# Eight expert jobs as one pipeline over the job borders, with the outputs kept in DRAM by slot

## What is computed

```python
logits = (ht @ w_router).astype(jnp.float32)
top_logits, top_idx = lax.top_k(logits, TOP_K)          # TOP_K = 2 of N_EXPERTS = 8
top_w = jax.nn.softmax(top_logits, axis=-1)
combine = jnp.sum(jax.nn.one_hot(top_idx, N_EXPERTS) * top_w[..., None], axis=1)
for e in range(N_EXPERTS):
    y = swiglu(ht, w_gate[e], w_up[e], w_down[e])       # (silu(h @ w_gate) * (h @ w_up)) @ w_down
    out = out + combine[:, e:e + 1] * y
```

## Time and profile before

| | |
|---|---|
| device time, median of 3 (lowest to highest) | 1696.33 us (1695.38 to 1701.48) |
| the profiled execution, from its first to its last instruction | 1695.6 us |
| what lies around that span in the median | 0.7 us |
| TensorE busy | 1564.9 us (92%) |
| VectorE busy | 1245.4 us (73%) |
| ScalarE busy | 1017.5 us (60%) |
| GpSimd busy | 79.7 us (5%) |
| bytes moved | 446.03 MB, 263 GB/s over the span |
| mean granted TensorE clock | 0.962 of full speed |

### The profile page before, as it was taken

One profiled execution on the slowest core, in us unless ns is written; L12 is line 12 of the kernel. 1 busy time (PEld: TensorE's weight loads), 2 busy tenths in 40 slices (PEclk: granted clock), 3 DMA queues, 4 the chain that ended last, 5 costly groups with the idle time before them and its releaser, 6 DMA issues.

```text
span 1695.6 us, 22769 instructions
## 1 busy us (share of the span) xinstructions
PE 1564.9 (92%) x8311; PEld 1308.0 (77%) x8311; DVE 1245.4 (73%) x1044; ACT 1017.5 (60%) x949; POOL 79.7 (5%) x89
## 2 busy tenths in 40 slices
PE   5888999998987877999999999999999999999996
PEld 4777888878986866887887887887887887887885
DVE  4745555545674446888888888888888888888886
ACT  4444434334853334677677677677777777777774
POOL 0002000000223112000000000000000000000000
PEclk9789999999999796999999999999999999999999
DMA  9317655552430212999999999999999999999992
GB/s 329 98 39 275 220 174 194 176 174 100 133 117 28 75 62 97 347 361 351 344 368 349 336 387 337 345 372 344 341 369 351 336 374 349 341 372 339 361 368 88
DMA packets 190790, 446.03 MB, mean 263 GB/s; under 512 B 9632, under 2 KB 10016, under 8 KB 190752
## 3 DMA queue, kind: packets, MB, share of 16 engines
q1 hardware_dynamic: 184032, 430.83, 71.1%
q0 software_dynamic: 3456, 12.58, 1.9%
q10 hardware_dynamic: 3264, 2.08, 0.4%
HBM read 436.03 MB, written 9.44 MB: 263 GB/s over the span
## 4 chain that ended last, share of the span: by engine, by line
PE 84%; DVE 6%; ACT 5%; issue 3%; ACTq 1%; DVEq 1%; POOL 0%; POOLq 0%
PE PS L283 25%; PE PS L285 25%; PE PS L284 25%; DVE w_low L275 2%; ACT w_high L271 2%; PE PS L1277 1%; PE PS L846 1%; PE PS L920 1%; PE PS L1162 1%; ACT xs L520 1%; ACT L271 1%; PE PS L896 0%; PE PS L1153 0%; PE PS L1209 0%; PE PS L909 0%
## 5 line engine op out<-in xcount | busy, mean ns | idle before, releaser
L275 DVE TENSOR_TENSOR w_low<-w_raw,w_high 128x2048 fp32r<-128x2048 f32 x408 | 934.0, 2296 | 247.6 <-ACT w_high L271 247.4
L271 ACT ACTIVATE w_high<-w_raw 128x2048 fp32r<-128x2048 f32 x408 | 781.2, 1917 | 393.9 <-PE PS L285 393.0
L283 PE MATMUL PS<-w_high,x_high 128*128 128x512 f32 x1264 | 503.5, 398 | 23.7 <-DVE pickT L1838 15.1
L285 PE MATMUL PS<-w_high,x_low 128*128 128x512 f32 x1264 | 495.6, 392 | 0.0
L284 PE MATMUL PS<-w_low,x_high 128*128 128x512 f32 x1264 | 494.9, 392 | 0.0
L283 PEld LDWEIGHTS PS<-w_high,x_high 128*128 128x128 f32 x1264 | 239.5, 189 | 76.8 <-DVE w_low L275 22.4
L285 PEld LDWEIGHTS PS<-w_high,x_low 128*128 128x128 f32 x1264 | 238.8, 189 | 51.5
L284 PEld LDWEIGHTS PS<-w_low,x_high 128*128 128x128 f32 x1264 | 239.4, 189 | 48.4
L283 PE MATMUL PS<-w_high,m_act_high 128*128 128x512 f32 x448 | 177.9, 397 | 11.9 <-DVE m_act_low L1831 11.9
L285 PE MATMUL PS<-w_high,m_act_low 128*128 128x512 f32 x448 | 177.2, 395 | 0.0
L284 PE MATMUL PS<-w_low,m_act_high 128*128 128x512 f32 x448 | 177.1, 395 | 0.0
(11 more groups left out here) (271 smaller groups left out, 1364.9 us busy)
## 6 DMA issues: line engine op xcount, KB each, us to landing
w_raw<-in_m_w_gate SPq DMA_DIRECT2D x112, 1024.0 KB, 7.2
w_raw<-in_m_w_up SPq DMA_DIRECT2D x112, 1024.0 KB, 7.1
w_raw<-in_m_w_down SPq DMA_DIRECT2D x112, 1024.0 KB, 6.7
w_raw<-in_b_w_in SPq DMA_DIRECT2D x16, 1024.0 KB, 5.5
w_raw<-in_f_w_gate SPq DMA_DIRECT2D x14, 1024.0 KB, 5.1
w_raw<-in_f_w_up SPq DMA_DIRECT2D x14, 1024.0 KB, 5.1
w_raw<-in_f_w_down SPq DMA_DIRECT2D x14, 1024.0 KB, 4.9
w_raw<-in_a_w_qkv SPq DMA_DIRECT2D x6, 1024.0 KB, 13.9
```

What stands on the lines that cost most here:

```text
L271: nc.scalar.activation(WH[:, n % SPLIT, :], W[:, n % RAW, :], ACT.Copy).then_inc(hi_done, 1)
L275: nc.vector.tensor_tensor(WL[:, n % SPLIT, :], W[:, n % RAW, :], WH[:, n % SPLIT, :].bitcast(f32), ALU.subtract).then_inc(lo_done, 1)
L283: nc.tensor.matmul(o, sH, mH, start=first, stop=False)
L285: return nc.tensor.matmul(o, sL, mH, start=False, stop=last)
```

## The change

The eight jobs become one sequence of 56 chunks, numbered q over all jobs. TensorE does the gate and up of chunk q+1 between the turning and the down of chunk q everywhere but at the end, so over the job borders too. For this the rows of the next job are turned in chunk 5 of a job, after the last up that needs the old ones.

A job's output is no longer carried back by matmuls. ScalarE copies the PSUM banks 2 and 3 to a tile (`y_slots`, `y_out`) in the first chunk of the next job, and GpSimd stores the 512 KB to a DRAM scratch by slot (`y_slots_dram`). In the last job GpSimd gathers each token's two rows with four indirect DMAs (`y_tokens`), and VectorE adds them to `h` with four instructions of 128 x 1024. The last job, whose output isn't stored, and jobs beyond the eighth, if there are any, still go through `back` and `add`. Scratch rows that no stored job writes are cleared with five more stores of zeros, beside the twelve that clear the x scratch. The first up no longer waits for `pickT`, and the reading of `njobs` and its tests come after the eighth job.

```diff
@@ -193,12 +193,17 @@
             w_fin = sb("w_fin", [128, D], c=c)
             m_gain = sb("m_gain", [128, D], c=c)
             xg = sb("x_slots", [128, D], c=c)
+            ys = sb("y_slots", [128, D], c=c)
+            yg = sb("y_tokens", [128, 2, TT, D], c=c)
             late, row_e, row_s = (sb(n, R8, c=c) for n in ("late", "row_e", "row_s"))
             offs = sb("offs", [128, E], c=c)
             rowf = sb("rowf", [128, 2, TT], c=c)
             slot = sb("slot", [128, 2, TT], u32, c=c)
         xw = fin
         x_dram = nc.dram_tensor("x_slots_dram", ((JOBS + 1) * 128, D), f32, kind="Internal").ap()
+        y_dram = nc.dram_tensor("y_slots_dram", ((JOBS + 1) * 128, D), f32, kind="Internal").ap()
+        LAST = E - 1
+        Y_CLEAR = JOBS + 1 - LAST
...
+                def inner(j):
+                    with sp.Fori(0, NC - 1) as i:
+                        gate_up(n0 + 4, j * NC + i, j, ds((i + 1) * CH, CH))
+                        down(n0 + 8, j * NC + i, j, i)
+
+                gate_up(n0, 0, 0, slice(0, CH))
+                with sp.Fori(0, LAST) as j:
+                    inner(j)
+                    gate_up(n0 + 4, j * NC + NC - 1, j + 1, slice(0, CH))
+                    down(n0 + 8, j * NC + NC - 1, j, NC - 1)
+                inner(LAST)
+                down(n0 + 4, E * NC - 1, LAST, NC - 1)
...
+                for j in range(LAST, JOBS + 1):
+                    pool.dma_start(y_dram[128 * j:128 * j + 128, :], zeros[:]).then_inc(sem("y_stored"), 16)
...
+                def store(j):
+                    pool.wait_ge(sem("ys_out"), j + 1)
+                    pool.dma_start(y_dram[ds(j * 128, 128), :], ys[:]).then_inc(sem("y_stored"), 16)
+
+                with pool.Fori(0, LAST - 1) as j:
+                    pool.wait_ge(sem("gather_ps"), j + 2)
+                    pool.dma_start(xg[:], x_dram[ds((j + 2) * 128, 128), :]).then_inc(sem("xg_in"), 16)
+                    store(j)
+                store(LAST - 1)
+                pool.wait_ge(sem("y_stored"), 16 * (Y_CLEAR + LAST))
+                for c in range(2):
+                    for t in range(TT):
+                        nc.gpsimd.indirect_dma_start(yg[:, c, t], None, y_dram[:, :], bass.IndirectOffsetOnAxis(ap=slot[:, c, t:t + 1], axis=0))\
+                            .then_inc(sem("yg_in"), 16)
...
+                def y_out(j):
+                    act.wait_ge(w_used, n0 + 4 + (j + 1) * NC * RAW)
+                    act.wait_ge(sem("y_stored"), 16 * Y_CLEAR + 16 * j)
+                    nc.scalar.activation(ys[:].rearrange("p (b n) -> p b n", b=2), PS[:, 2:4, :], ACT.Copy).then_inc(sem("ys_out"), 1)
+
+                def y_high(n, r):
+                    act.wait_ge(w_used, n + r * RAW)
+                    nc.scalar.activation(ysH[:].rearrange("p (b n) -> p b n", b=2), PS[:, 2:4, :], ACT.Copy)\
+                        .then_inc(sem("ys_high"), 1)
...
+                def step(q, out_of=None, x_of=None):
+                    split_high(act, n0 + 6, q)
+                    if out_of is not None:
+                        y_out(out_of)
+                    split_high(act, n0 + 7, q)
+                    turned(q)
+                    split_high(act, n0 + 8, q)
+                    act.wait_ge(sem("m_act_done"), q + 1)
+                    silu(n0 + 6, q)
+                    split_high(act, n0 + 9, q)
+                    if x_of is not None:
+                        turned_in(x_of)
+                    split_high(act, n0 + 10, q)
+                    split_high(act, n0 + 11, q)
+
+                split_high(act, n0 + 3)
+                silu(n0 + 2, 0)
+                split_high(act, n0 + 4)
+                split_high(act, n0 + 5)
+                step(0)
+                with act.Fori(0, LAST) as j:
+                    with act.Fori(1, NC - 2) as i:
+                        step(j * NC + i)
+                    step(j * NC + NC - 2, x_of=j + 1)
+                    step(j * NC + NC - 1)
+                    step(j * NC + NC, out_of=j)
+                with act.Fori(LAST * NC + 1, E * NC - 1) as q:
+                    step(q)
+                turned(E * NC - 1)
+                y_high(n0 + 6, E * NC - 1)
...
+                def step(q, first=False, final=False, x_of=None, x_wait=None, out_of=None):
+                    pe.wait_ge(sem("m_silu_done"), q + 1)
+                    if x_wait is not None:
+                        pe.wait_ge(sem("gather_low"), x_wait + 1)
+                    gate(n0 + 4, q)
+                    pe.wait_ge(sem("m_act_done"), q + 1)
+                    turned()
+                    up(n0 + 6, q)
+                    if x_of is not None:
+                        turn_in(x_of)
+                    pe.wait_ge(sem("m_low_done"), q + 1)
+                    if out_of is not None:
+                        pe.wait_ge(sem("ys_out"), out_of + 1)
+                    down(n0 + 8, q, first, final)
+
                 gather(0)
+                pe.wait_ge(sem("gather_low"), 1)
+                gate(n0, 0)
+                pe.wait_ge(sem("slot_done"), 1)
+                up(n0 + 2, 0)
+                step(0, first=True)
+                with pe.Fori(0, LAST) as j:
+                    with pe.Fori(1, NC - 2) as i:
+                        step(j * NC + i)
+                    step(j * NC + NC - 2, x_of=j + 1)
+                    step(j * NC + NC - 1, final=True, x_wait=j + 1)
+                    step(j * NC + NC, first=True, out_of=j)
+                with pe.Fori(LAST * NC + 1, E * NC - 1) as q:
+                    step(q)
+                pick_turned(1)
+                pe.wait_ge(sem("m_act_done"), E * NC)
+                turned()
+                pe.wait_ge(sem("m_low_done"), E * NC)
+                down(n0 + 4, E * NC - 1, False, True)
+                back(0)
...
@@ -1771,6 +1872,7 @@
                                                       op0=ALU.mult, op1=ALU.subtract)
                     last.then_inc(sem("gather_low"), 1)
 
+                split_low(dve, n0 + 2)
                 gathered(0)
 
                 def turned_in(j):
...
+                def step(q, x_of=None):
+                    split_low(dve, n0 + 6, q)
+                    split_low(dve, n0 + 7, q)
+                    turned(q)
+                    split_low(dve, n0 + 8, q)
+                    split_low(dve, n0 + 9, q)
+                    gated(q + 1, n0 + 8, q)
+                    if x_of is not None:
+                        turned_in(x_of)
+                    split_low(dve, n0 + 10, q)
+                    split_low(dve, n0 + 11, q)
+
+                split_low(dve, n0 + 3)
+                split_low(dve, n0 + 4)
+                gated(0, n0 + 4, 0)
+                split_low(dve, n0 + 5)
+                step(0)
+                with dve.Fori(0, LAST) as j:
+                    with dve.Fori(1, NC - 2) as i:
+                        step(j * NC + i)
+                    step(j * NC + NC - 2, x_of=j + 1)
+                    step(j * NC + NC - 1)
+                    step(j * NC + NC)
+                picks(LAST, slice(0, 128))
+                with dve.Fori(LAST * NC + 1, E * NC - 1) as q:
+                    step(q)
+                turned(E * NC - 1)
+                pick_turned(0)
+                dve.wait_ge(sem("yg_in"), 16 * 2 * TT)
+                for c, weight in enumerate((w0, w1)):
+                    for t in range(TT):
+                        if c:
+                            dve.wait_ge(sem("added"), t + 1)
+                        V.scalar_tensor_tensor(out=h[:, t], in0=yg[:, c, t], scalar=weight[:, t:t + 1], in1=h[:, t],
+                                               op0=ALU.mult, op1=ALU.add).then_inc(sem("added"), 1)
+                dve.sem_inc(sem("added"), 4 * LAST)
+                y_low(0)
+                add(0, LAST)
```

More of the change, by code:

```diff
@@ L343, in job, with of_expert, gate_up, down @@
                                lambda i: j * NC + i)
-                with sp.Fori(0, E) as j:
-                    job(j, j)
+                n0 = base["moe"]
+                def of_expert(w, e):
+                    return w[0, ds(e, 1)].rearrange("a (k p) c -> p (a k) c", p=128)
+                def gate_up(n, r, e, col):
+                    for i, w in enumerate((m_w_gate, m_w_up)):
+                        for half in range(2):
+                            fetch(sp, n + 2 * i + half, r, "cols", of_expert(w, e)[:, 4 * half:4 * half + 4, col])
+                def down(n, r, e, c):
+                    for half in range(2):
+                        fetch(sp, n + half, r, "rows", of_expert(m_w_down, e)[:, ds(4 * c + 2 * half, 2), :])
+                def inner(j):
[9 more added lines that the diff above has]
+                down(n0 + 4, E * NC - 1, LAST, NC - 1)
                 sp.wait_ge(sem("jobs_done"), 1)
@@ L1306, in turn_in, with pick_turned, gate, up @@
                     last.then_inc(sem("gather_ps"), 1)
-                gather(0)
+                def pick_turned(c):
```

(43 more changed lines are left out.)

138 lines of the change are left out of this document (51 added, 87 removed).

## The result

| | before | after |
|---|---|---|
| median of 4 runs each, beside each other (lowest to highest) | 1697.85 us (1695.38 to 1701.48) | 1648.18 us (1645.92 to 1650.57) |
| profiled execution, span | 1695.6 us | 1646.1 us |
| TensorE busy | 1564.9 us (92%) | 1542.3 us (94%) |
| bytes moved | 446.03 MB | 453.97 MB |
| mean granted clock | 0.962 | 0.957 |

The ratio is 0.9712, with a 95% interval from 0.9698 to 0.9726. The kernel is 2.9% faster. The forecast of 1646.8 us lies 1.4 us under the median and within the lowest and highest run.

What follows compares the result with a forecast made beforehand. TensorE was taken as the bound, waiting only at job borders, on small dependent steps and not loads. Savings of 43.6 + 6.3 + 0.6 - 1.0 = 49.5 us took the median from 1696.33 to 1646.8 us; range 1640 to 1661 us.

Steps and rivals of the forecast that it cites:

- Seven borders: Job borders inside the stage: a job takes 119.93 us instead of 126.16, so seven borders save 43.6 us.
- the stall in chunk 5: TensorE waiting on VectorE's `w_low` after the next job's rows are turned: 0.2 us a border, bounds 0 and 1.0.
- the chain: Chunk 5: transposes, ScalarE's two copies and split, then VectorE's split, ending at 720.5 us; TensorE needs the block at 720.55.
- `y_out` at nothing: ScalarE's 1.03 us output copy in the next chunk but one delays a split some 0.2 us, covered by VectorE: no cost.
- The start: First gate matmul to first turning: 19.9 us instead of 26.23, saving 6.3 us.
- The end: Last turning and tail: transposes no longer stand before the last turning, two small matmuls do; 0.6 us saved.
- The gathers: Last job: four gathers of 0.52 MB delay weight loads; cost taken as 1.0 us, between 0 and 5.7.
- The room of 4.5 us for late loads: Slack of weight loads: a block has 12.6 us, loads land in 7.5 us, at most 8.1.
- The DMA bound at 371 GB/s: Rival over all jobs: DMAs can move no more, so a job takes 121.6 us, the kernel 1659 us; chance 0.19.
- The mean rate of 353: Rival over whole jobs: only 353 GB/s can be held, a job takes 127.7 us, the kernel 1700 us; chance 0.04.
- The fetch at the jump back: Rival at the loop's end: seven jumps fetch instructions at 3.4 us each, 24 us in all, 1671 us; chance 0.04.
- The signs: Expected if right: 119.7 to 120.2 us between transposes, `pickT` matmuls only in last job, clock 1.00 from 672 us, landing below 9.

## Why the prediction held, step by step

- **Seven borders, forecast 43.6 us.** Measured 7 x (126.16 - 119.72) = 45.1 us. The transposes cost the 0.87 us counted: a job of 119.72 us is 0.86 more than seven chunks. The 0.2 us for the stall in chunk 5 were not paid: 0.19 us of cover remain where I had none. From the start of the transposes to the end of VectorE's split the chain had 6.42 us, the trace has 782.83 - 776.54 = 6.29; TensorE comes back after 6.48, where I had 6.47. The doubled copies show that the chain is the right one.
- **`y_out` at nothing.** Right; another 1.03 us there is free too.
- **The start, forecast 6.3 us.** Measured 26.23 - 19.91 = 6.3 us. One reason given for it is wrong: the first gate is slow not because TensorE comes out of a wait. By the run with dummy matmuls the clock was at 0.50 before that wait, under busy matmuls. The sum doesn't hang on it, since it takes the 8.37 us as they are.
- **The end, forecast 0.6 us.** It came out as a loss of 0.4 us. The transposes left the last border, so the last turning comes 11.67 us after the one before it, where it was 12.38: 0.7 us saved. VectorE's four instructions end at 1628.1, before `ys_high` at 1628.95: hidden, as counted. It was not seen that the last `back` could run at the lower clock: behind the same idle of 2.37 us its matmuls are 0.43 us apart in this profile, and 0.23 in that of before. It costs 1.5 us, so the tail behind the last turning is 1.1 us longer; where the clock stayed full it is some 0.4 us shorter than before (23.66 us in the unchanged kernel's second profile). This term, taken at nothing, is the one that the sum lacks. With the same idle time ahead, the profiles without the DRAM route and with the output's copy made twice show the half too, and those of the unchanged kernel run again, of the second store and of the copies to `x_high` made twice the full clock, so it differs from execution to execution. It isn't simply a matter of coming back slow: in the profile without the DRAM route the clock is 1.00 from 1632.74 to 1633.20 us, over the first two matmuls behind the idle time, and 0.50 from 1633.30 on.
- **The gathers, forecast 1.0 us.** Measured 0.57 us in this profile, and 0, 0.16, 0.68 and 1.12 us in four others with the same gathers and one store. The room of 4.5 us for late loads was about the right size: landing rose by 6 us, and ScalarE waited four times, 4.7 us in all, for a load, of which 0.3 us came through to TensorE as a wait. What I had not seen is that the backlog stays: loads up to 1600 us landed in 9.1 us or more. A reason that fits: the last job has no store and no rows to load, so a chunk wants 6 x 1.049 MB in 16.97 us, 371 of the 393 GB/s that moved with a backlog, which leaves 6%.
- **The rivals.** The DMA bound at 371 GB/s would have shown in every border; a job moves 377, and 383 with a second store. The mean rate of 353 falls with it. By the figure of the Trainium skill, "DMA: Bandwidth & Descriptors", Bandwidth, that the HBM side gives a core about 358 GB/s, a job would take an estimated 126 us; the trace differs, by 377 GB/s over a whole job. What the prediction left out is that the same section calls about 358 GB/s the share of a core when both cores of the HBM domain stream, and gives up to 425 GB/s for one alone; the 377 GB/s of this single core agree with that. The fetch at the jump back would be idle time at the loop's end; TensorE shows none there, with 312 matmuls in the body (before there were 246, not the 247 of the prediction).
- **The signs.** 119.72 us from transposes to transposes, the clock at 1.00 from 672 us on, and `pickT` only at the end came as said. Landing times below 9 us did not: up to 9.2 us before the gathers, and 13.9 behind them. ScalarE waited for loads behind the gathers, which the prediction named as the DMA rival's sign; its price is the 0.57 us, and it is absent at the borders.
- **Not foreseen:** the first gate came 0.87 us later, from stages that the change hardly touches. In the profiles of this study it lies between 664.0 and 669.3 us, so this is no effect of the change.

The terms that were off, +1.5 us at the borders, +0.4 us at the gathers, -0.9 us ahead of the first gate and -1.0 us at the end (0.6 forecast, -0.4 measured), cancel. That the profiled span came out at just the 1646.1 us of the forecast is chance by some 2 us.

## What to carry to other kernels

A border between equal jobs costs the sum of its small dependent waits, and removing the longest one shows the next: here it gave 2.6 of 6.4 us, and the rest came only when work of the neighbouring job was laid over the border and the table loads left it. Before adding work to a helper engine, read in the timeline when its product is next wanted: about 1 us on ScalarE cost 0.95 us in one chunk and nothing two chunks later. Where TensorE must wait anyway, matmuls that nobody reads can bring its clock up. Put at two places they made this kernel 4.4 us faster by the medians, to 1640.74 us, the lowest median here. The profiles show 2.9 us of it at the first place. At the second they could save 1.5 us where the clock would be at the half, which is not shown: both profiles with them have the full clock, but so have three of the six without.

## What the runs showed of the hardware

- TensorE was granted half its clock (0.50) from 657.0 to 660.8 us, while busy in all of it with 128x128 f32 matmuls. Ten 128x512 ones began at 660.85; the clock was 0.50 up to 664.0, 0.73 over the next 1.5 us and 1.00 from 665.5 us. Behind a gap of 2.37 us the clock was full for the eight matmuls in three profiles; in the others it was half from the first (one profile) or fell behind the first or second of them (two).
- One core moved 377 GB/s over a job of 119.8 us, and with a backlog of loads 404 GB/s over 18 us and 393 over 55 us.
- Of four indirect gathers of 128 rows of 4 KB in a row, the first held GpSimd 1.2 to 3.1 us and each of the others 2.3 to 2.5; with one in a chunk it was 1.1 to 1.7 us:

```profile
L444 POOL DMA_INDIRECT y_tokens<-y_slots_dram,slot x4: 1149/1666/1702, 1538.3 to 1588.6; - x4
```

- From 1545 to 1600 us, behind four in a row, the weight loads landed in 9.1 us or more (8.6 with the dummy matmuls). With one in a chunk they were late too, 9.5 us or more; without gathers they landed in 5.5 to 8.0 us.
